# A transformer and hybrid block on one core: POOL's second feed-forward block waits for DVE's last low row, and the last stage's rows and second weight block are moved

## The chip, the cores and the metric

One core of a Trainium2 chip. The metric is the device time of one execution in microseconds; three executions of the kernel before took 4351.44, 4353.88 and 4355.54 us (median 4353.88). Engines: PE (TensorE, matmul), PEld (its weight load), DVE (VectorE), ACT (ScalarE), POOL (GpSimd) and SP (SyncE, here a queue of loads only).

## The reference

Input x has 512 tokens of 1024 channels, fp32. Four layers come first, each a mixer (hyena, window attention, pool, hyena) and a feed-forward:

```python
x = x + y
x = x + swiglu(rmsnorm(x, norm_ffn[i]), ff_w_gate[i], ff_w_up[i], ff_w_down[i])
# swiglu: (silu(xn @ wg) * (xn @ wu)) @ wd, hidden width 2816
```

Then one block with gated delta rule heads and latent attention, merged, and at its end a modulated squared-relu MLP:

```python
x = x + mod_x[5] * _sq_relu_mlp(_modulate(_rms(x, norm_mlp[l]), mod_x[3], mod_x[4]), w_mlp_in[l], w_mlp_out[l])
# _modulate(xn, shift, scale) = xn * (1.0 + scale) + shift;  _sq_relu_mlp: square(relu(h @ w1)) @ w2
```

## The kernel before, in words

x lies in SBUF with channels on the partitions: DT = 8 rows of [128, 512]. All stages follow one list (hyena, feed-forward and so on); each engine has its own program over that list, in which every instruction is issued in order and waits on semaphores. The order is written out by hand.

**Split products.** The large layers are computed with two rounded parts of each operand. A value v has a high part (v rounded to fp32r) and a low part (v less the high part), and PE adds three matmuls per tile pair (`split_product`, L954 to L956; `split_pair` L965 to L967 for a stage's first block): high weights times high rows, high weights times low rows, low weights times high rows. Weights come in blocks of [128, 2048] (output blocks are narrower) through a ring of four slots, loaded by SP (L597) as slots come free. For each block ACT copies the ring slot into `w_hi` (`split`, L1891), then POOL subtracts into `w_lo` (L808), both with two buffers, chosen by j % 2; PE waits for `wlo_set` before it uses the block. SP's load for a slot waits for the `wlo_set` of the block that was in it.

**A feed-forward's start.** The mixer's last layer writes eight output tiles. For each, DVE adds the tile to x (`residual`: L2565, L2567 or L2569), ACT makes the high row `x_hi` with the norm's gain (L1911, Identity with a per-partition scale) and the square for the norm (L1907), DVE the low row `x_lo` (`scaled_low`, L2502, a scalar_tensor_tensor, signals `xn_set`) and the running sum of the squares (`fold`, L2534). Behind its squares 4 and 5 ACT issues the split of the stage's weight blocks 0 and 1 (L1926, L1928). POOL splits block 0 as soon as its high part is there. Block 1 (j == 1) also waits until PE has finished the mixer's last tile (`acc_full`). DVE's last instructions are: the last tile into x, low row 6, low row 7, the fold of square 6.

PE goes through the first block row by row, two tiles side by side, six matmuls a row, and waits for `xn_set` at each row. Behind row 2 it issues the column sums of the squares (L927 on the folded tile, which waits for the last fold, and L931), behind row 5 the spread of the norm's factor over the tokens (L938).

**The last stage** (`modulate(1)`, then `mlp`). The output layer of the merge runs 16 matmuls a tile (L918), `gated_residual` (L3293) adds each tile to x, ACT takes the squares, with the split of block 0 behind square 4. There is no fold of the gain here: the factor must be known before the rows. So the column sums, the root and the spread come first; then DVE makes for each row k the product with gain and factor (L2880, scalar_tensor_tensor), adds the shift in place (L2881, tensor_scalar), ACT copies the high row (L1898, signals `xhi_set`), and DVE subtracts for the low row of k - 1 (`low`, L2497). ACT's program issues the split of block 1 only at the start of `mlp` (L2428), behind its eight high rows:

```python
for f in range(DT):
    if f % 2 == 0:
        ends.append(acc.n + 2)
        j += 1
        split("mlp", 0, j)
    t = full(acc, acc_full)
```

From then on each input block lasts 48 matmuls on PE, each output block 24, and ACT and POOL prepare the next one meanwhile.

Of the kernel before, what the change touches and what calls it, by code (L numbers as in the profile page):

```python
# [18 lines left out]
DT = D // P  # L19
# [270 lines left out]
def build_program(nc, stream, vecs, tabs, tabs2, x_in, ctx_in, first_mods, scratch, x_keep, diag, solved_t, solved_n, out, schedule):  # L290
# [4 lines left out]
    with ExitStack() as stack:  # L295
# [450 lines left out]
        def _(pool):  # L746
# [50 lines left out]
            def split(stage, blocks_):  # L797

                def run_(arg):
                    first = starts[(stage, arg)]  # L800
                    for j in range(blocks_):
                        k = first + j
                        cols = blocks[k][2]
                        n["split"] += 1
                        pool.wait_ge(whi_set, n["split"])
                        if stage == "ffn" and j == 1:
                            pool.wait_ge(acc_full, n["acc"])
                        nc.gpsimd.tensor_tensor(w_lo[:, j % 2, 0:cols], ring[:, k % RING, 0:cols], w_hi[:, j % 2, 0:cols],  # L808
                                                ALU.subtract).then_inc(wlo_set, 1)
                    if stage == "ffn":  # L810
                        n["aux"] += 2
                        n["acc"] += 2 * (FT + DT)
                return run_
# [1039 lines left out]
        def _(act):  # L1853
# [59 lines left out]
            def norm(gain, then=None):  # L1913

                first = acc.n - DT
                if gain is not None and gain[0] == "norm_ffn":
                    then = ("ffn", gain[1] // DT)
                ffn_next = gain is not None and gain[0] == "norm_ffn"
                for k in range(n["squared"], DT):
                    if ffn_next:  # L1920
                        scaled(k, first + k, gain)
                    if first >= 0:
                        square(k, first + k)
                    else:
                        signal(go(xn[:, k, :], x[:, k, :], ACT.Square), squares_set)
                    if then and k == 4:  # L1926
                        split(*then, 0)
                    if k == 5 and ffn_next:  # L1928
                        split(*then, 1)
                    if k == DT - 2 and first >= 0 and split_target(gain) == "hyena":  # L1930
                        high_weights(starts[("hyena", gain[1] // DT // 3)], in_hi[0])
                    if k == DT - 2 and split_target(gain) == "attention":
                        high_weights(starts[("attention", 0)], at_whi[:, 0, :])
                n["squared"] = 0
                step(go(small_t[:, 26:27], one_col, ACT.Sqrt))
                t = aux.take()
                aux.take()
                act.wait_ge(aux_drained[aux.place(t)], aux.turn(t) + 1)
                signal(go(rstd_col, rstd_col, ACT.Sqrt, bias=eps_col, scale=1.0 / D), root_set)
                if split_target(gain) == "hyena":  # L1940
                    if first < 0:
                        high_weights(starts[("hyena", gain[1] // DT // 3)], in_hi[0])
                    split_x(x_hi_h)
                if split_target(gain) == "attention":
                    split_x(x_hi_a)
                if then and not ffn_next:
                    split_x(x_hi)

            def ffn(layer):
                n["xn"] += DT  # L1950
# [469 lines left out]
            def mlp(_):  # L2420
                ends.clear()
                j = 0
                for part in range(4):
                    for f in range(DT):
                        if f % 2 == 0:
                            ends.append(acc.n + 2)
                            j += 1
                            split("mlp", 0, j)  # L2428
                        t = full(acc, acc_full)
                        if f >= 2:  # L2430
                            act.wait_ge(hidden_set, DEPTH * FT + DT * part + f - 1)
                        drain(go(h_tmp[:, f % 2, :], bank(t)[:], ACT.Relu), t)
                    for m in range(DT):
                        acc.n += 1
                        ends.append(acc.n)
                        j += 1
                        if j < 6 * DT:
                            split("mlp", 0, j)
# [25 lines left out]
        def _(dve):  # L2464
# [34 lines left out]
            def scaled_low(k, gain):  # L2499
                n["xhi"] += 1  # L2500
                dve.wait_ge(xhi_set, n["xhi"])
                signal(stt(x_lo[:, k, :], x[:, k, :], V(gain[0], gain[1] + k), x_hi[:, k, :], ALU.mult, ALU.subtract), xn_set)  # L2502

            def split_hidden(f):

# [365 lines left out]
            def modulate(which):  # L2871
# [5 lines left out]
                    step(tt_(gm[:, c, :], gm[:, c, :], gain, ALU.mult))  # L2877
                t, rows = rstd_rows()
                for k in range(DT):
                    step(stt(xn[:, k, :], x[:, k, :], gm[:, 0, k:k + 1], rows, ALU.mult, ALU.mult))  # L2880
                    signal(ts_(xn[:, k, :], xn[:, k, :], modv[:, shift + k, 0:1], None, ALU.add), plain_set if which else xn_set)  # L2881
                    if which and k:
                        low(k - 1)
                rows_read(t)
                if which:
                    low(DT - 1)
                n["xn"] += DT
                if which == 0:
                    n["sq"] += DT
# [661 lines left out]
```

## Time and profile before

| what | value |
| --- | --- |
| median of three executions | 4353.88 us |
| the profiled execution | 4356.94 us |
| its span in the profile | 4355.1 us |
| mean granted clock of PE | 0.953 of full speed |
| PE busy | 4128.2 us (95%) |
| DVE busy | 2225.0 us (51%) |
| POOL busy | 1495.2 us (34%) |
| ACT busy | 1270.7 us (29%) |

Busy times are sums over the whole span. PE's matmuls overlap, so its busy time is not work at its peak, and stretches in which its granted clock is low count as busy as well. The feed-forwards start near 448, 1073, 1492 and 2285 us, the last stage's block 0 at 3984 us.

### The profile page before, as it was taken

The numbers are of one execution on the slowest core, as the hardware profiler recorded it, in microseconds if no ns is written. First come the engines' busy times: TensorE is split into PE (matmuls) and PEld (weight loads), VectorE is DVE, ScalarE is ACT, GpSimd is POOL, SyncE is SP. The second block draws the span as 40 slices with busy tenths as digits, with TensorE's granted clock in tenths as the row PEclk, the third lists the DMA queues.
The fourth block names the chain that finished last, engine by engine and source line by source line (L and its number), as shares of the span: only waits on it lengthen the run. The fifth ranks groups of instructions, "written<-read, shape, count | busy, mean of one in ns | idle before, by whom it ended". The sixth has DMA issues, their size and how long they took to land.

```text
span 4355.1 us, 48965 instructions
## 1 busy us (share of the span) xinstructions
PE 4128.2 (95%) x19446; PEld 3130.2 (72%) x19446; DVE 2225.0 (51%) x3169; ACT 1270.7 (29%) x1756; POOL 1495.2 (34%) x845
## 2 busy tenths in 40 slices
PE   7998999999999999999989999899999999998999
PEld 6655888777888888876568886566666665775887
DVE  6588435476514441575875244556663356404322
ACT  3332222355222322233322222323221234412222
POOL 3311344321444244433124441466663000331343
PEclk9998999999999899999989998989998889999999
DMA  6201332311232223222013321111111111221222
GB/s 184 98 29 39 110 108 82 111 46 55 95 118 83 85 79 120 92 71 94 29 49 124 116 80 66 43 41 54 39 36 54 70 72 65 78 93 62 92 103 76
DMA packets 101075, 341.94 MB, mean 79 GB/s; under 512 B 44400, under 2 KB 47600, under 8 KB 72176
## 3 DMA queue, kind: packets, MB, share of 16 engines
q1 hardware_dynamic: 87968, 311.60, 20.5%
q10 hardware_dynamic: 12880, 27.20, 2.2%
q8 instruction: 155, 2.54, 0.2%
q14 instruction: 72, 0.59, 0.0%
HBM read 321.48 MB, written 17.30 MB: 78 GB/s over the span
## 4 chain that ended last, share of the span: by engine, by line
PE 83%; DVE 11%; ACT 2%; POOL 2%; issue 1%; DMA 0%; SPq 0%; DVEq 0%; ACTq 0%; POOLq 0%
PE bank L954 17%; PE bank L955 17%; PE bank L956 17%; PE bank L1454 5%; PE bank L1166 2%; PE bank L1078 1%; PE bank L1434 1%; PE bank L1156 1%; PE bank L1074 1%; PE bank L918 1%; PE bank L1755 1%; PE bank L1754 1%; PE bank L1776 1%; PE bank L1686 1%; PE bank L1715 1%
## 5 line engine op out<-in xcount | busy, mean ns | idle before, releaser
L808 POOL TENSOR_TENSOR w_lo<-ring,w_hi 128x2048 fp32r<-128x2048 f32 (+2 forms) x200 | 776.2, 3881 | 1214.6 <-ACT w_hi L1891 1193.9
L954 PE MATMUL bank<-x_hi,w_hi 128*128 128x512 f32 x1584 | 617.7, 390 | 7.5 <-POOL w_lo L808 7.5
L956 PE MATMUL bank<-x_hi,w_lo 128*128 128x512 f32 x1584 | 616.6, 389 | 0.0
L955 PE MATMUL bank<-x_lo,w_hi 128*128 128x512 f32 x1584 | 616.4, 389 | 0.0
L1891 ACT ACTIVATE w_hi<-ring 128x2048 fp32r<-128x2048 f32 (+2 forms) x200 | 322.0, 1610 | 712.9 <-PE bank L956 712.0
L954 PE MATMUL bank<-h_hi,w_hi 128*128 128x512 f32 x960 | 374.0, 390 | 0.4
L955 PE MATMUL bank<-h_lo,w_hi 128*128 128x512 f32 x960 | 373.6, 389 | 0.0
L956 PE MATMUL bank<-h_hi,w_lo 128*128 128x512 f32 x960 | 373.5, 389 | 0.0
L954 PEld LDWEIGHTS bank<-x_hi,w_hi 128*128 128x128 f32 x1584 | 297.4, 188 | 70.2 <-POOL w_lo L808 9.2
L956 PEld LDWEIGHTS bank<-x_hi,w_lo 128*128 128x128 f32 x1584 | 297.4, 188 | 61.9
L955 PEld LDWEIGHTS bank<-x_lo,w_hi 128*128 128x128 f32 x1584 | 297.4, 188 | 61.6
L821 POOL TENSOR_TENSOR ring_r<-ring,merge_hi 128x2048 fp32r<-128x2048 f32 x16 | 73.3, 4584 | 497.4 <-ACT merge_hi L2403 497.4
L1454 PE MATMUL bank<-xn,ring 128*128 128x512 f32 x496 | 238.9, 620 | 1.4 <-DVE work L2924 1.4
L2569 DVE TENSOR_TENSOR x<-bank,x 128x512 f32<-128x512 f32 x72 | 49.8, 692 | 356.8 <-PE bank L956 345.3
L954 PEld LDWEIGHTS bank<-h_hi,w_hi 128*128 128x128 f32 x960 | 180.2, 188 | 39.3 <-DVE h_lo L2508 2.1
L956 PEld LDWEIGHTS bank<-h_hi,w_lo 128*128 128x128 f32 x960 | 180.3, 188 | 37.5
L955 PEld LDWEIGHTS bank<-h_lo,w_hi 128*128 128x128 f32 x960 | 180.2, 188 | 37.1
L1966 ACT ACTIVATE xn<-xn 128x512 f32<-128x512 f32 x88 | 55.7, 633 | 455.9 <-DVE xn L2582 455.8
L793 POOL TENSOR_TENSOR tab<-tab 56x31 f32<-56x31 f32 (+15 forms) x248 | 155.1, 626 | 19.4
L2582 DVE TENSOR_TENSOR xn<-bank,rstd_t 128x512 f32<-128x512 f32 x88 | 60.8, 691 | 194.0 <-PE bank L956 187.3
L1454 PEld LDWEIGHTS bank<-xn,ring 128*128 128x128 f32 x496 | 92.6, 200 | 89.9 <-issue 88.7
L845 POOL TENSOR_TENSOR work<-work,ring 128x1024 f32<-128x1024 f32 x32 | 76.8, 2432 | 228.4 <-DVE x L2635 171.6
(527 smaller groups left out, 7934.0 us busy)
## 6 DMA issues: line engine op xcount, KB each, us to landing
ring<-stream SPq DMA_DIRECT2D x211, 1024.0 KB, 4.8
ring<-stream SPq DMA_DIRECT2D x64, 704.0 KB, 4.0
ring<-stream SPq DMA_DIRECT2D x36, 512.0 KB, 3.4
xn<-first_mods SPq DMA_DIRECT2D x8, 1024.0 KB, 6.9
x<-x_keep ACTq DMA_DIRECT2D x3, 2048.0 KB, 8.8
ring<-stream SPq DMA_DIRECT2D x4, 1088.0 KB, 4.9
bias_rows<-work ACTq DMA_DIRECT2D x1, 4096.0 KB, 46.5
x_keep<-x ACTq DMA_DIRECT2D x2, 2048.0 KB, 10.8
```

Of the source, the lines that this page charges most:

```text
L793: solve(tt(W[:, 0:i, i:SUB], W[:, 0:i, i:SUB], part, ALU.subtract))
L808: nc.gpsimd.tensor_tensor(w_lo[:, j % 2, 0:cols], ring[:, k % RING, 0:cols], w_hi[:, j % 2, 0:cols], ALU.subtract).then_inc(wlo_set, 1)
L821: nc.gpsimd.tensor_tensor(ring_r[:, w, 0:2 * DT * P], ring[:, w, 0:2 * DT * P], merge_whi[j % 2][:], ALU.subtract).then_inc(wlo_set, 1)
L845: nc.gpsimd.tensor_tensor(pair, pair, factor[:, r:r + 1, :].broadcast_to([P, 2, 512]), ALU.mult).then_inc(filt_set, 1)
L954: mm(b[:], hi[:, at + k, :], rhs_hi, start=(k == 0), stop=False)
L955: mm(b[:], hi[:, at + k, :], rhs_lo[:, k, :], start=False, stop=False)
L956: ins = mm(b[:], lo[:, at + k, :], rhs_hi, start=False, stop=(k == kt - 1))
L1166: ins = mm(b[:], fwd[term], filt[:, kind, term[1], :], start=(j == 0), stop=(j == 1))
L1454: ins = mm(b[:, 0:TC] if ctx else b[:], w[:, at + k, :], src[:, k, :], start=(k == 0), stop=(k == DT - 1))
L1891: signal(go(w_hi[:, j % 2, 0:cols], ring[:, k % RING, 0:cols], ACT.Copy), whi_set)
L1966: signal(go(gate_tmp[:, f % 2, :], gate_tmp[:, f % 2, :], ACT.Silu), silu_set)
L2582: drain(tt_(gate, bank(t)[:], rstd, ALU.mult), t)
```

## The change

Four edits. POOL's split of block 1 of each feed-forward waits in addition for all low rows of that layer (`xn_set` at 8 * (2 * layer + 2)). In the last stage ACT's split of block 1 is issued behind square 5 of the residual, as in the feed-forwards, and no longer at the start of `mlp`. DVE no longer adds the shift: ACT's high row is an Identity activation with the shift as its bias, rounded to fp32r, and DVE's low row is a scalar_tensor_tensor (row plus shift, less the high row). `modulate(0)` keeps its two instructions a row.

```diff
--- before.py
+++ after.py
@@ -805,6 +805,7 @@
                         pool.wait_ge(whi_set, n["split"])
                         if stage == "ffn" and j == 1:
                             pool.wait_ge(acc_full, n["acc"])
+                            pool.wait_ge(xn_set, DT * (2 * arg + 2))
                         nc.gpsimd.tensor_tensor(w_lo[:, j % 2, 0:cols], ring[:, k % RING, 0:cols], w_hi[:, j % 2, 0:cols],
                                                 ALU.subtract).then_inc(wlo_set, 1)
                     if stage == "ffn":
@@ -1925,7 +1926,7 @@
                         signal(go(xn[:, k, :], x[:, k, :], ACT.Square), squares_set)
                     if then and k == 4:
                         split(*then, 0)
-                    if k == 5 and ffn_next:
+                    if k == 5 and then:
                         split(*then, 1)
                     if k == DT - 2 and first >= 0 and split_target(gain) == "hyena":
                         high_weights(starts[("hyena", gain[1] // DT // 3)], in_hi[0])
@@ -1944,7 +1945,10 @@
                 if split_target(gain) == "attention":
                     split_x(x_hi_a)
                 if then and not ffn_next:
-                    split_x(x_hi)
+                    for k in range(DT):
+                        n["plain"] += 1
+                        act.wait_ge(plain_set, n["plain"])
+                        signal(go(x_hi[:, k, :], xn[:, k, :], ACT.Identity, bias=modv[:, 3 * DT + k, 0:1]), xhi_set)
 
             def ffn(layer):
                 n["xn"] += DT
@@ -2425,7 +2429,8 @@
                         if f % 2 == 0:
                             ends.append(acc.n + 2)
                             j += 1
-                            split("mlp", 0, j)
+                            if j > 1:
+                                split("mlp", 0, j)
                         t = full(acc, acc_full)
                         if f >= 2:
                             act.wait_ge(hidden_set, DEPTH * FT + DT * part + f - 1)
@@ -2500,6 +2505,11 @@
                 n["xhi"] += 1
                 dve.wait_ge(xhi_set, n["xhi"])
                 signal(stt(x_lo[:, k, :], x[:, k, :], V(gain[0], gain[1] + k), x_hi[:, k, :], ALU.mult, ALU.subtract), xn_set)
+
+            def shifted_low(k, shift):
+                n["xhi"] += 1
+                dve.wait_ge(xhi_set, n["xhi"])
+                signal(stt(x_lo[:, k, :], xn[:, k, :], modv[:, shift + k, 0:1], x_hi[:, k, :], ALU.add, ALU.subtract), xn_set)
 
             def split_hidden(f):
 
@@ -2877,13 +2887,17 @@
                     step(tt_(gm[:, c, :], gm[:, c, :], gain, ALU.mult))
                 t, rows = rstd_rows()
                 for k in range(DT):
-                    step(stt(xn[:, k, :], x[:, k, :], gm[:, 0, k:k + 1], rows, ALU.mult, ALU.mult))
-                    signal(ts_(xn[:, k, :], xn[:, k, :], modv[:, shift + k, 0:1], None, ALU.add), plain_set if which else xn_set)
-                    if which and k:
-                        low(k - 1)
+                    ins = stt(xn[:, k, :], x[:, k, :], gm[:, 0, k:k + 1], rows, ALU.mult, ALU.mult)
+                    if which:
+                        signal(ins, plain_set)
+                        if k:
+                            shifted_low(k - 1, shift)
+                    else:
+                        step(ins)
+                        signal(ts_(xn[:, k, :], xn[:, k, :], modv[:, shift + k, 0:1], None, ALU.add), xn_set)
                 rows_read(t)
                 if which:
-                    low(DT - 1)
+                    shifted_low(DT - 1, shift)
                 n["xn"] += DT
                 if which == 0:
                     n["sq"] += DT
```

## Rows read from the trace of the kernel before

**Rows 1.** Page, part 4: the chain that ended last, shares of the span by engine.
```profile
PE 83%; DVE 11%; ACT 2%; POOL 2%; issue 1%; DMA 0%; SPq 0%; DVEq 0%; ACTq 0%; POOLq 0%
```
**Rows 2.** What PE waited for: us in total, times, longest us.
```profile
PE bank L927 <- DVE xn L2534: 34.5, 10, 15.9
...
PE bank L954 <- POOL w_lo L808: 7.5, 4, 3.5
```
**Rows 3.** Timeline of PE at three feed-forward starts: start us, us, instruction [idle before].
```profile
452.11 0.39 PE L967 MATMUL bank<-x_hi,w_lo 128*128 128x512 f32 x1
455.69 1.02 PE L927 MATMUL bank<-ones,xn 128*128 128x1 f32 x8 [3.19 <-DVE xn L2534]
...
1499.58 1.02 PE L927 MATMUL bank<-ones,xn 128*128 128x1 f32 x8 [1.35 <-DVE xn L2534]
...
2291.80 1.02 PE L927 MATMUL bank<-ones,xn 128*128 128x1 f32 x8 [2.87 <-DVE xn L2534]
```
**Rows 4.** Stretches: length, busy us per engine, granted clock, DMA share, GB/s.
```profile
457.50:461.20 3.70, 3.70 (x11) 2.89 (x12) 0.50 (x3) 0.30 (x1) 0.00 (x0) 0.54 0.34 102
...
2653.00:3731.00 1078.00, 992.55 (x5784) 689.28 (x5783) 601.99 (x1326) 325.23 (x621) 377.83 (x549) 0.90 0.17 53
...
3952.00:3958.50 6.50, 6.50 (x16) 2.85 (x15) 1.44 (x2) 2.54 (x2) 2.09 (x1) 1.00 0.00 0
...
4002.60:4021.00 18.40, 18.39 (x81) 15.21 (x82) 12.29 (x13) 3.72 (x4) 9.43 (x2) 1.00 0.17 58
```
**Rows 5.** Timeline of DVE at the first feed-forward start.
```profile
443.71 0.75 DVE L2502 SCALAR_TENSOR_TENSOR x_lo<-x,vec,x_hi 128x512 fp32r<-128x512 f32 x1
...
449.29 5.52 DVE L2502 SCALAR_TENSOR_TENSOR x_lo<-x,vec,x_hi 128x512 fp32r<-128x512 f32 x2
454.85 0.69 DVE L2534 TENSOR_TENSOR xn<-xn 128x512 f32<-128x512 f32 x1
```
**Rows 6.** Timeline of POOL at the first feed-forward start.
```profile
448.89 4.59 POOL L808 TENSOR_TENSOR w_lo<-ring,w_hi 128x2048 fp32r<-128x2048 f32 x1 [7.62 <-PE bank L956]
```
**Rows 7.** Chain in order of time, last stage's start: start us, us, what.
```profile
3980.50 0.76 DVE xn L2880
...
3983.84 0.76 DVE xn L2880
3984.62 0.50 DVE xn L2881
3985.14 0.70 DVE x_lo L2497
...
3996.03 1.93 ACT w_hi L1891
3998.03 4.54 POOL w_lo L808
```
**Rows 8.** Timeline of PE at the last stage's start.
```profile
3983.95 0.77 PE L965 MATMUL bank<-x_hi,w_hi 128*128 128x512 f32 x1 [3.55 <-DVE x_lo L2497]
...
4002.61 0.50 PE L954 MATMUL bank<-x_hi,w_hi 128*128 128x512 f32 x1 [3.53 <-POOL w_lo L808]
```
**Rows 9.** ACT's groups by shape: busy us, mean ns.
```profile
L1911 ACT ACTIVATE x_hi<-x,vec 128x512 fp32r<-128x512 f32 x32 | 23.2, 724 | 46.1 <-DVE x L2567 26.3 <-DVE x L2565 12.1 <-DVE x L2569 7.4
```
**Rows 10.** Timeline of DVE, a feed-forward start and a head's stage.
```profile
1095.79 0.69 DVE L2508 TENSOR_TENSOR h_lo<-xn,h_hi 128x512 fp32r<-128x512 f32 x1
...
2905.05 0.74 DVE L2997 SCALAR_TENSOR_TENSOR work<-bank,work 128x128 f32<-128x128 f32 x2
2905.82 0.62 DVE L2965 TENSOR_SCALAR work<-work,vec 128x772 f32<-128x772 f32 x1
```
**Rows 11.** Timeline of POOL at the same two places.
```profile
1095.81 5.16 POOL L808 TENSOR_TENSOR w_lo<-ring,w_hi 128x2048 fp32r<-128x2048 f32 x1 [17.74 <-ACT w_hi L1891]
...
2905.94 1.64 POOL L783 TENSOR_TENSOR x<-x,tab 128x512 f32<-128x512 f32 x1 [14.60 <-DVE work L2997]
```
**Rows 12.** Timeline of ACT ahead of the last stage.
```profile
3967.49 0.63 ACT L1907 ACTIVATE xn<-x 128x512 f32<-128x512 f32 x1 [6.24 <-DVE x L3293]
```

## The prediction

> **What bounds the kernel now.** The page comes first. The chain that ended last is 83% PE and 11% DVE [rows 1], so a microsecond is worth something only where PE has nothing to issue or runs at half clock. The list of PE's waits names the two places that the change touches [rows 2]: L927, the first matmul of the column sums, has waited 34.5 us for DVE's fold (L2534) in ten places, and L954, the product on a low weight block, 7.5 us for POOL in four.
>
> The timeline of PE splits the first sum [rows 3]. The ten include the four feed-forward starts, each after 18 matmuls of the first block: 3.19, 2.84, 1.35 and 2.87 us, together 10.25. Behind each wait PE falls to half clock: at the first start the granted clock is 0.54 from 457.5 to 461.2 us, which is almost all 1.2 instead of 2.4 GHz [rows 4].
>
> DVE's timeline says why the fold is late [rows 5]. A low row (L2502) takes 0.75 us undisturbed (443.71), but the pair at 449.29 takes 5.52, and the fold only starts at 454.85. POOL's timeline gives the holder: its split of block 1 (L808) starts at 448.89 and takes 4.59, to 453.48 [rows 6]; the two operations with both inputs in SBUF don't run together. The same pattern stands at the other three starts.
>
> In the last stage the chain shows DVE at three instructions a row and then, in series, ACT's high part of block 1 (3996.03), POOL's low part (3998.03, 4.54) and PE's L954 at 4002.61, which has waited 3.53 us [rows 7, 8].
>
> **Feed-forward starts, four times: the added wait.** It keeps POOL off until low row 7 is written. Worked out at the first start: low row 6 runs 449.29 to 450.04. ACT's high row 7 cannot start before x is written at 449.26; with 0.72 us for an L1911 [rows 9] and about 0.06 for each hand-over it ends near 450.07, low row 7 runs 450.13 to 450.88, the fold 450.92 to 451.61. PE issues its 18th matmul at 452.11 and is free at about 452.35 [rows 3], 0.7 us after the fold. So all of the wait goes; the third start, with the shortest wait, has over 2 us of room by the same working. Gain: 10.25.
>
> What queues behind the new wait: on POOL only the splits of blocks 2 and later, whose high parts come 18 us later. Block 1 would be done at about 451 + 5.2 = 456.2. PE needs it after 30 more matmuls, the column sums and the spread: before at 466.9, now near 462 (an estimate, 466.9 less the gain below). SP's fifth load waits for that split too, but PE uses that block some 40 us on (each block lasts 48 times 0.23, 11 us). The cover is 5 us; without it each microsecond of lateness would cost one.
>
> **Who takes the port.** The new risk is the moment itself: low row 7 releases POOL's 4.6 us split and DVE's own fold together. Nearest rows [rows 10, 11]: L2997 ended at 2905.79, DVE's next instruction started at 2905.82 and the one of POOL that waited for L2997 at 2905.94, so DVE was first by 0.12. Six hand-overs in this trace are of this kind and all leave DVE ahead by 0.1; in nine others POOL starts 0.06 to 0.09 after the end of DVE's instruction, and DVE's own next, where nothing else holds it, comes after 0.04. With a lead of only 0.02 (1095.79 against 1095.81) DVE kept its 0.69 us and POOL took 5.16 instead of 4.6. I take: the fold first, POOL 0.6 longer, at no cost; both ends stay (rival B).
>
> **The clock behind the waits.** Eight or nine matmuls step 0.43 instead of 0.23 us after each of the four column sums; at the first start 457.5 to 461.2 holds 3.7 us of half clock [rows 4], in which half the time is lost: about 1.7; the others measure 1.55, 1.5 and 1.57 by the same count. Sum 6.3. Will it go? The column sums themselves (1.8 us of one-column matmuls) remain, the idle time before them does not. Below: nothing is regained, 0. Above: 6.3. For the upper end speaks that PE stood still for 3.53 us at 3999 and still had a granted clock of 1.00 afterwards [rows 4, 8]; against it, that at the third start 1.35 us of waiting plus the sums was enough. What stood before each of the four falls was the wait and the sums; with the wait gone only the sums are left. I take 6.3, the value of the rows on which PE keeps working.
>
> **Last stage, the rows.** Now: L2880 0.75, L2881 0.49, L2497 0.69 and gaps, 1.93 in work and 2.03 us a row with three gaps [rows 7]. After: L2880 0.75 and a scalar_tensor_tensor with two SBUF inputs for the low row; the nearest row is L2502 at 0.75 [rows 5]. With two gaps of 0.04 that is 1.57 a row. ACT's copy becomes an Identity with a per-partition operand, 0.72 as L1911 [rows 9]: it fits into 1.57. The profile's table loads stand at six lines, and none is an Identity's, so none is added. Start: L2880 of row 0 ends at 3981.25, ACT 3981.34 to 3982.06, low row 0 3982.12 to 3982.87, PE from 3983.02 instead of 3983.95 [rows 8]. Low rows then end 1.57 apart, row 7 near 3993.3. PE, at half clock for its first seven matmuls as now (3.1 us), one step of 0.27, then 40 of 0.2275, is free at 3995.5; its row 6 would begin at 3992.8, low row 6 is ready at 3992.5. So PE, not DVE, bounds this piece by 0.3 us; before, it was free at about 3999, 4002.61 less the wait.
>
> **Last stage, block 1.** Its high part now goes into ACT's gap behind the sixth square: ACT stands idle 6.24 us before 3967.49 [rows 12], and 3961.3 + 1.9 = 3963.2. The block has landed by then: the second output block releases its slot, and no DMA moves from 3952 to 3958.5 [rows 4]; the next load is that of block 2. POOL has it at 3967.8. It may hold the fold that starts at 3967.43 for 0.4 us, which the 5.4 us to the next tile hide. So PE goes from block 0 to block 1 at 3995.5 instead of 4002.61: 7.1, where 3.5 is the floor (the wait alone) and 7.5 the ceiling. Block 2 follows: ACT from about 3996.9, POOL done by 4003.5, PE needs it at 4006.4.
>
> **Sum.** 10.25 + 6.3 + 7.1 = 23.7 us off the profiled execution's 4356.94 (span 4355.1, 1.8 around it): 4333.2. That execution lies 3.06 above the median of the three shown; against 4353.88 it is 4330.2.
>
> **Rivals.**
> A, the clock stays low: only the waits go. For it speaks the third start, against it the idle 3.53 us without a fall. Gain 10.25 + 7.1 = 17.4: 4336.5. The Trainium skill, "TensorE: Matmul & The Clock Gate", Part 1, has the clock follow how busy PE has been; by that rule the sums alone might not hold the clock up, and this rival is what it would give. No row here has the sums without a wait before them.
> B, POOL gets the port before the fold. Then the fold ends 0.7 after a split that starts at 450.97 and ends at 455.57: 456.3 against 455.54 now. By the same working the four starts lose 0.75 + 1.0 + 1.05 + 1.05 = 3.9, the last stage keeps its 7.1: 4350.7. It decides if POOL is released less than 0.04 us after DVE's row; [rows 10, 11] speak against it. The Trainium skill, "SBUF — State Buffer", section "SBUF: two separate sides", has the one that starts first hold the shared port pair for its whole instruction. By that rule either order is possible here and the second pays the whole of the other's time; the trace agrees with the rule (5.52 for two rows of 0.75 behind a running split), and what decides between B and the main case is the 0.04 alone.
> C, the wait does nothing (the count is already reached at its place): only the 7.1 remains, 4346.8. The count of the rows, 16 a layer, speaks against it.
> D, slower: the half clock of the heads' stages. From 2653 to 3731 the granted clock is 0.90 [rows 4], so some 215 of 1078 us run at half clock, by bursts and waits whose place moves with everything before. To turn 23.7 of gain into a loss over 8.7, 32 us must come from there, which is 65 more us at half clock, granted clock 0.87 instead of 0.90. That point is 4363. The three times shown lie within 4.1 us, which speaks against such a swing.
>
> **How the numbers follow.** Main case 0.74, A 0.13, B 0.07, C 0.03, D 0.03. The range from 4325 (a low row a little cheaper, the runs' own scatter of 4 us) to 4342 holds the main case and A with that scatter; B, C and D are left out. A measurement can tell 0.2%, 8.7 us: the main case and A are faster, B and C the same, D slower.
>
> **What would show it.** After: at the four starts L927 has no wait for L2534, the two L2502 at the end 0.75 each, the fold 0.69 and the split behind it near 5.2; the matmuls after the column sums 0.23 apart (A: 0.43). L2880 followed by a low row every 1.57 us; the second split near 3963; L954 of block 1 without a wait for POOL. Wrong would be a fold of 4 us or more (B), a split beside the last low rows as now (C), or a longer stretch from 2653 to 3731 with a lower granted clock (D).

## The result and the profile after

The kernel takes 4323.15 us (median of three executions, 4320.36 to 4326.44) against 4353.88: a ratio of 0.9931 [0.9917, 0.9944], 30.7 us less. The forecast was 23.7 us less, 4330.2, with a range from 4325; the direction and the mechanism came out as forecast, the size did not: the time lies below the range. The profiled execution took 4323.15 us, its span is 4321.3 us, PE's mean granted clock 0.957 (before 0.953). Two executions of the experiments, 8133.07 us (the kernel before, experiment 10) and 7977.36 us (one of the eleven of experiment 6), took nearly twice as long as all the others and enter no ratio below.

The names of the lines move: L927 is now L928, L954 is L955 and L965 L966, the low row of a feed-forward L2507, the fold L2544, POOL's split L809, the last stage's product L2890 and its new low row L2512.

The chain of the page (part 4), of the changed kernel, against [rows 1]: PE has a point more of it, DVE a point less.

```profile
PE 84%; DVE 10%; ACT 2%; POOL 2%; issue 1%; DMA 0%; SPq 0%; DVEq 0%; ACTq 0%; POOLq 0%
```

PE's waits in the changed kernel (us in total, times, longest us), against [rows 2]:

```profile
PE bank L928 <- DVE xn L2544: 23.9, 6, 15.5
...
PE bank L955 <- POOL w_lo L809: 3.9, 3, 1.3
...
PE bank L966 <- DVE x_lo L2512: 2.7, 1, 2.7
```

The column sums waited 34.5 us in ten places and now 23.9 in six: the four feed-forward starts have left the list. The low weights cost 7.5 us in four places and now 3.9 in three; the longest, 3.5, is gone.

At the first start, DVE's timeline (start us, us, instruction, in brackets the idle time before it and what ended it), against [rows 5], with the second start behind it:

```profile
443.26 0.75 DVE L2577 SCALAR_TENSOR_TENSOR x<-bank,vec,x 128x512 f32<-128x512 f32 x1 [3.33 <-PE bank L957]
444.05 1.64 DVE L2507 SCALAR_TENSOR_TENSOR x_lo<-x,vec,x_hi 128x512 fp32r<-128x512 f32 x2
445.72 0.69 DVE L2544 TENSOR_TENSOR xn<-xn 128x512 f32<-128x512 f32 x1
...
1065.51 1.64 DVE L2507 SCALAR_TENSOR_TENSOR x_lo<-x,vec,x_hi 128x512 fp32r<-128x512 f32 x2
1067.18 0.69 DVE L2544 TENSOR_TENSOR xn<-xn 128x512 f32<-128x512 f32 x1
```

POOL's timeline at the same two starts, against [rows 6], and at the last stage:

```profile
446.21 4.65 POOL L809 TENSOR_TENSOR w_lo<-ring,w_hi 128x2048 fp32r<-128x2048 f32 x1 [10.20 <-DVE x_lo L2507]
...
1067.31 4.99 POOL L809 TENSOR_TENSOR w_lo<-ring,w_hi 128x2048 fp32r<-128x2048 f32 x1 [4.28 <-DVE x_lo L2507]
...
3936.35 4.52 POOL L809 TENSOR_TENSOR w_lo<-ring,w_hi 128x2048 fp32r<-128x2048 f32 x1 [2.35 <-ACT w_hi L1892]
```

The last pair of low rows takes 1.64 instead of 5.52 us and the fold follows at once. The last low row ends at 1067.15 at the second start; the fold starts 0.03 later and POOL 0.16 later, and the fold keeps its 0.69; it is POOL's split that stretches (4.99 against 4.59). At the first start POOL comes about 0.5 behind and hardly stretches.

PE's timeline at the first start, against [rows 3]: no bracket on the column sums, which follow the 18th product directly, and steps of 0.23 us behind them.

```profile
446.85 0.39 PE L968 MATMUL bank<-x_hi,w_lo 128*128 128x512 f32 x1
447.08 0.94 PE L928 MATMUL bank<-ones,xn 128*128 128x1 f32 x8
447.89 1.03 PE L932 MATMUL bank<-ones,xn 128*128 128x1 f32 x8
448.78 0.48 PE L966 MATMUL bank<-x_hi,w_hi 128*128 128x512 f32 x1
449.10 0.39 PE L967 MATMUL bank<-x_lo,w_hi 128*128 128x512 f32 x1
...
3956.13 0.77 PE L966 MATMUL bank<-x_hi,w_hi 128*128 128x512 f32 x1 [2.67 <-DVE x_lo L2512]
...
3969.04 0.39 PE L955 MATMUL bank<-x_hi,w_hi 128*128 128x512 f32 x1
```

The last two of these rows are the last stage: the start waits 2.67 us instead of 3.55, and block 1 follows block 0 without the 3.53 us of [rows 8]. Stretches of the changed kernel (length, busy us of PE, PEld, DVE, ACT and POOL, granted clock, DMA share, GB/s): the column sums and what follows at the first start, then block 0 of the last stage in two parts.

```profile
447.00:449.00 2.00, 2.00 (x19) 1.96 (x18) 0.00 (x0) 0.01 (x1) 2.00 (x1) 1.00 0.19 78
449.00:452.60 3.60, 3.60 (x17) 2.93 (x17) 0.50 (x3) 0.30 (x1) 1.86 (x1) 1.00 0.43 109
3956.10:3960.10 4.00, 3.97 (x9) 3.15 (x10) 3.82 (x6) 1.54 (x3) 0.00 (x0) 0.50 0.00 0
3960.10:3969.00 8.90, 8.90 (x40) 7.39 (x39) 5.91 (x9) 3.18 (x5) 0.00 (x0) 0.99 0.00 0
```

At the first start the clock stays at 1.00 (2.4 GHz), where it was 0.54 before [rows 4]. Block 0 of the last stage still has its cold beginning, 4.0 us at 1.2 GHz.

DVE's rows in the last stage, changed kernel, against [rows 7]: product and low row, one pair every 1.57 us.

```profile
3955.24 0.75 DVE L2512 SCALAR_TENSOR_TENSOR x_lo<-xn,modv,x_hi 128x512 fp32r<-128x512 f32 x1
3956.02 0.75 DVE L2890 SCALAR_TENSOR_TENSOR xn<-x,gm,bank 128x512 f32<-128x512 f32 x1
3956.81 0.75 DVE L2512 SCALAR_TENSOR_TENSOR x_lo<-xn,modv,x_hi 128x512 fp32r<-128x512 f32 x1
```

**Where the time went.** PE issues the same 19,446 matmuls in every trace here (a kernel with spare matmuls has these more), so two traces can be laid side by side by the number of the matmul. A start is the stretch from the first matmul of a feed-forward's block 0 to the matmul 114 later. Worked out from the records of the two traces, in us:

| stretch | before | after |
| --- | --- | --- |
| up to start 1 | 432.35 | 427.47 |
| start 1 | 28.19 | 23.16 |
| start 2 | 27.86 | 23.16 |
| start 3 | 27.86 | 24.75 |
| start 4 | 27.89 | 23.20 |
| the rest of each of the four feed-forwards | 342.37 | 342.37 |
| norm and attention mixer | 254.36 | 255.99 |
| norm and pool mixer | 49.11 | 49.01 |
| norm and second hyena | 421.97 | 421.89 |
| norm ahead of the heads | 5.75 | 5.04 |
| heads' stage | 591.16 | 586.26 |
| merge's output layer and norm | 65.75 | 64.85 |
| last stage, block 0 until block 1 | 18.66 | 12.91 |
| the rest of the last stage | 343.64 | 343.41 |

The four starts lose 17.5 us and the last stage 6.9 (0.90, 5.75 and 0.23), 24.4 in all, near the forecast 23.7. But these two executions lie 33.8 us apart, and the medians 30.7. The other 9.4 come mostly from two stretches in which the change does nothing, 4.9 each: the way to the first start and the heads' stage. (The stretch left out of the table, between the heads and the merge's output layer, agrees within 0.01, and the wait ahead of the first matmul differs by 0.36.) So either the change acts there in some hidden way, or a single trace isn't a fair sample. That is what the experiments had to settle.

### The profile page after: what moved, and what is told of

Read it like the earlier page. It is cut to its first block, busy times and chain, and to the rows that moved or that the text cites. A ratio compares the mean times of both kernels' runs of the same rounds, so it can differ in the third digit from the quotient of the medians.

```text
span 4321.3 us, 48957 instructions
## 1 busy us (share of the span) xinstructions
PE 4112.0 (95%) x19446; PEld 3121.2 (72%) x19446; DVE 2201.9 (51%) x3161; ACT 1271.4 (29%) x1756; POOL 1495.7 (35%) x845
## 3 DMA queue, kind: packets, MB, share of 16 engines
q8 instruction: 155, 2.54, 0.2%
## 4 chain that ended last, share of the span: by engine, by line
PE 84%; DVE 10%; ACT 2%; POOL 2%; issue 1%; DMA 0%; SPq 0%; DVEq 0%; ACTq 0%; POOLq 0%
PE bank L955 17%; PE bank L956 17%; PE bank L957 17%; PE bank L1455 5%; PE bank L1167 2%; PE bank L1079 1%; PE bank L1435 1%; PE bank L1157 1%; PE bank L1075 1%; PE bank L919 1%; PE bank L1756 1%; PE bank L1755 1%; PE bank L1777 1%; PE bank L1687 1%; PE bank L1716 1%
## 5 line engine op out<-in xcount | busy, mean ns | idle before, releaser
L809 POOL TENSOR_TENSOR w_lo<-ring,w_hi 128x2048 fp32r<-128x2048 f32 (+2 forms) x200 | 776.9, 3885 | 1189.4 <-ACT w_hi L1892 1158.5
L955 PE MATMUL bank<-x_hi,w_hi 128*128 128x512 f32 x1584 | 617.4, 390 | 3.9 <-POOL w_lo L809 3.9
L955 PE MATMUL bank<-h_hi,w_hi 128*128 128x512 f32 x960 | 373.9, 389 | 0.4
L955 PEld LDWEIGHTS bank<-x_hi,w_hi 128*128 128x128 f32 x1584 | 297.4, 188 | 66.2 <-POOL w_lo L809 5.2
L955 PEld LDWEIGHTS bank<-h_hi,w_hi 128*128 128x128 f32 x960 | 180.2, 188 | 39.3 <-DVE h_lo L2518 2.0
L2866 DVE SCALAR_TENSOR_TENSOR kbuf<-xn,vec,kbuf 128x256 f32<-128x256 f32 x112 | 154.0, 1416 | 2.0
```

The lines of the kernel that those rows point to most:

```text
L955: mm(b[:], hi[:, at + k, :], rhs_hi, start=(k == 0), stop=False)
L2866: ins = stt(part, w[:, :, j, :], V("cond", 2 * j + c), part, ALU.mult, ALU.add)
```

## Experiments

Ratios are against the kernel before, measured beside them on the same chip, with a 95% interval in brackets; a number in brackets behind a time is the number of executions; "starts" is the sum of the four stretches of the table.

**1. The changed kernel again.** No edit.

> The changed kernel, a second time, unchanged. Theory 1 (the 7 us beyond the forecast 23.7 are the runs' own scatter in stages that the change does not touch, where PE falls to half clock at other places from one execution to the next): the ratio over five rounds comes to between 0.9935 and 0.9950 (22 to 28 us), and in the trace the 448 us ahead of the first feed-forward, where no instruction is changed, take anything between 443 and 449 us. Theory 2 (the surplus belongs to the change): the ratio stays near 0.993 (30 us) and the stages between the feed-forward starts are again shorter than in the trace before by the same amounts.

Measured: 4321.46 us (5 executions), the kernel before 4352.49 (21): 0.9927 [0.9915, 0.9940], 31.0 us less. Starts 95.1. But up to the first start its trace takes 432.43 us, as much as the first trace of before, and norm and pool mixer 42.20 instead of 49.01. The 4.9 us up to the first start are therefore scatter, and a single stretch of one execution can be off by 5 to 7 us for the same code. The ratio is below what theory 1 gives (0.9935 to 0.9950), and its interval leaves out the forecast's 0.9946: the surplus over the forecast is real, and only its place in the first two traces misled. In the pool mixer the rows show what differs, PE's clock. 12 us near the mixer's end in the first trace of the changed kernel, then the like in this one (columns as above), and what PE does behind them here:

```profile
1466.00:1478.00 12.00, 12.00 (x59) 12.00 (x58) 9.29 (x8) 7.08 (x7) 4.54 (x1) 0.50 0.01 1
...
1460.00:1472.00 12.00, 12.00 (x109) 12.00 (x110) 10.02 (x14) 8.27 (x12) 0.05 (x1) 1.00 0.05 20
...
1476.71 0.80 PE L966 MATMUL bank<-x_hi,w_hi 128*128 128x512 f32 x1 [2.54 <-POOL w_lo L809]
```

At full clock PE is through the mixer earlier and then waits 2.54 us for POOL's low part of block 0; at half clock it is later and waits for nothing.

**2. POOL's wait alone**, on the kernel before:

```diff
+                            pool.wait_ge(xn_set, DT * (2 * arg + 2))
```

> The kernel before with POOL's added wait alone. By the forecast's terms: 10.25 us of waiting and 6.3 us of half clock at the four feed-forward starts, 16.5 us, ratio 0.9962. If the clock term is worth nothing: 10.3 us, 0.9976. If the surplus of 7 us belongs to the feed-forwards: 23 us, 0.9947. In the trace the four starts have no wait of the column sums for the fold and no 0.43 us steps behind them.

Measured: 4325.61 us (5), 0.994 [0.9926, 0.9953], 26.9 us less [20.5 to 32.2]. Starts 95.5, all four without a wait for the fold. The forecast for this part was 16.5, outside the interval. The wait is the part that gives more than forecast; the 23 us that were named for a surplus in the feed-forwards fit (the starts of experiments 3, 4 and 10 sum to 118.3, which is 22.8 more than 95.5).

**3. Block 1's split moved alone:**

```diff
-                    if k == 5 and ffn_next:
+                    if k == 5 and then:
...
-                            split("mlp", 0, j)
+                            if j > 1:
+                                split("mlp", 0, j)
```

> The kernel before with only the last stage's second weight split behind the residual's sixth square. Its 3.53 us wait for POOL goes, DVE's pace stays 2.03 us a row: 3.6 us, ratio 0.9992, not told apart from no change by the time; in the trace PE goes from block 0 to block 1 without a wait. If the two edits of the last stage need each other, nothing is gained.

Measured: 4348.68 us (11), 0.9994 [0.9985, 1.0003], 3.8 us less, which the time alone doesn't tell from no change. In the trace block 0 takes 14.96 instead of 18.66, which is 3.7, the 3.53 of the wait and little more, as the floor of the forecast said. Its trace holds the surprise: the starts, whose code is that of before, sum to 118.4 us instead of 111.8. Its stretches around the second start (columns as above): PE stands still, then the column sums, then products, then the clock is back.

```profile
1074.00:1076.90 2.90, 0.06 (x2) 0.07 (x1) 2.65 (x3) 0.00 (x0) 0.66 (x1) 1.00 0.01 3
1076.90:1079.20 2.30, 2.30 (x16) 2.30 (x17) 0.00 (x0) 0.00 (x0) 0.00 (x0) 0.74 0.00 0
1079.20:1084.90 5.70, 5.70 (x15) 4.50 (x16) 0.50 (x3) 0.30 (x1) 0.00 (x0) 0.51 0.55 213
1084.90:1090.00 5.10, 5.10 (x28) 4.32 (x27) 1.38 (x2) 0.00 (x0) 0.00 (x0) 1.00 0.90 376
```

The clock falls during the column sums already (0.74) and stays near 1.2 GHz for 5.7 us more: 12 steps of 0.43 us, where the first trace had 7 at this start. PE's timeline of the same place shows the sums themselves slowed: the second eight of them, 1.03 us in the first trace of after, take 1.64 here.

```profile
1076.86 1.02 PE L927 MATMUL bank<-ones,xn 128*128 128x1 f32 x8 [2.85 <-DVE xn L2535]
1077.75 1.64 PE L931 MATMUL bank<-ones,xn 128*128 128x1 f32 x8
```

**4. The shift alone:** ACT's high row with its bias and `shifted_low`, both as in the change, and neither the wait nor the moved split.

```diff
-                    split_x(x_hi)
+                    for k in range(DT):
...
+                        signal(go(x_hi[:, k, :], xn[:, k, :], ACT.Identity, bias=modv[:, 3 * DT + k, 0:1]), xhi_set)
```

> The kernel before with only the shift moved into ACT's rounding. Low rows every 1.57 us instead of 2.03; the last high row is done some 3.5 us earlier and ACT's and POOL's split of block 1 behind it as well, so PE starts block 1 3.6 us earlier, with the wait for POOL still about 3.5 us: 3.6 us, ratio 0.9992. If the chain through POOL hid all of it, 0.

Measured: 4347.75 us (11), 0.9990 [0.9981, 0.9998], 4.7 us less; in the trace 0.90 ahead of block 0 and 2.73 in it, 3.6. Its PE timeline in the last stage shows why no more: block 1 still waits for POOL.

```profile
3977.55 0.77 PE L965 MATMUL bank<-x_hi,w_hi 128*128 128x512 f32 x1 [2.67 <-DVE x_lo L2510]
...
3993.48 0.50 PE L954 MATMUL bank<-x_hi,w_hi 128*128 128x512 f32 x1 [2.85 <-POOL w_lo L808]
```

The two edits of the last stage remove different time (3.7 and 3.6; together 6.9), so neither stands in for the other. The starts here: 118.3. By their medians the three parts give 26.9 + 3.8 + 4.7 = 35.4 us, the whole 31.0; each of them is uncertain by some 4 to 6 us, so no interplay can be read from that.

**5. The clock without the wait's removal.** The kernel before, with 12 spare matmuls on tiles that are there already, issued ahead of the column sums, so that PE works while it waits. The fold is as late as before.

```diff
-            def column_sums():
+            def column_sums(fill=0):
...
+                for _ in range(fill):
+                    mm(b[:], w_hi[:, 0, 0:P], x_hi[:, 0, :], start=True, stop=True)
...
-                split_layers(2, FT // 2, FT // 2, True, {2: column_sums, 5: rstd_spread})
+                split_layers(2, FT // 2, FT // 2, True, {2: lambda: column_sums(12), 5: rstd_spread})
```

> The kernel before, POOL's split where it was, but PE issues 12 spare matmuls (2.7 us) into the column sums' bank while it waits for the fold at each of the four feed-forward starts. The wait's length stays, only PE's idle time is taken out of it, so the difference to the kernel before is the price of the clock alone (less 1.4 us at the third start, where the fill is longer than the wait). The forecast's clock term, 6.3 us in all: 5 us faster, ratio 0.9989. The rival that the first four single runs suggest (two traces without the wait added have 29.5, 31.2 and 29.5 us at starts 2 to 4 where the first trace has 27.9, half clock lasting 13 matmuls and not 8): 12 to 14 us faster, 0.997. If the column sums alone bring the clock down: no difference.

Measured: 4345.67 us (11), 0.9981 [0.9972, 0.9990], 8.5 us less [4.4 to 12.2], although the fold comes as late as before and no column sum starts more than 0.1 us earlier in its block. Starts 109.3 against 118.3. PE's timeline at the second start: the spare matmuls cover the wait, and the sums are not slowed.

```profile
1074.02 2.88 PE L925 MATMUL bank<-x_hi,w_hi 128*128 128x512 f32 x12
1076.98 1.05 PE L929 MATMUL bank<-ones,xn 128*128 128x1 f32 x8
1077.89 1.03 PE L933 MATMUL bank<-ones,xn 128*128 128x1 f32 x8
```

This is the clock's price by itself, and not all of it: at the first start 0.41 us of waiting is left and 7 slow steps follow, and at the third the spare matmuls last longer than the 1.35 to 1.68 us that they cover. By the time alone the 6.3 of the forecast is not excluded; the stretches are clearer. Starts 2 and 4, where the waits are covered, take 26.20 and 26.19 instead of 29.50 and 29.44: 3.3 us of clock each, where the forecast had 1.6.

**6. Rival B provoked.** The changed kernel, POOL released by low row 6 instead of 7:

```diff
-                            pool.wait_ge(xn_set, DT * (2 * arg + 2))
+                            pool.wait_ge(xn_set, DT * (2 * arg + 2) - 1)
```

> The changed kernel with POOL released by low row 6 instead of low row 7, so that its split is issued while row 7 runs and the fold comes behind it. If who is first at the port decides (rival B's mechanism), the fold takes 4.5 us or more at all four starts, the column sums wait again, and the time goes back by 20 us or more, to 4341 or above. If DVE's queued instruction keeps the port against POOL, the time stays at that of the changed kernel.

Measured: 4354.19 us (11; 4353.84 without the long one), 0.9997 [0.9987, 1.0006]: the starts' gain is gone. DVE's and POOL's timelines at the first start:

```profile
444.76 1.64 DVE L2507 SCALAR_TENSOR_TENSOR x_lo<-x,vec,x_hi 128x512 fp32r<-128x512 f32 x2
446.44 4.91 DVE L2544 TENSOR_TENSOR xn<-xn 128x512 f32<-128x512 f32 x1
```
```profile
446.04 4.76 POOL L809 TENSOR_TENSOR w_lo<-ring,w_hi 128x2048 fp32r<-128x2048 f32 x1 [9.30 <-DVE x_lo L2507]
```

Here the split began 0.40 us ahead of the fold, and the fold took 4.91 instead of 0.69: that is rival B. It is so at this start only. At the other three the split comes behind low row 6 and catches low row 7, and the fold behind it takes its 0.69. DVE's and POOL's timelines at the second start:

```profile
1070.94 5.13 DVE L2507 SCALAR_TENSOR_TENSOR x_lo<-x,vec,x_hi 128x512 fp32r<-128x512 f32 x1
1076.11 0.69 DVE L2544 TENSOR_TENSOR xn<-xn 128x512 f32<-128x512 f32 x1
```
```profile
1070.97 4.56 POOL L809 TENSOR_TENSOR w_lo<-ring,w_hi 128x2048 fp32r<-128x2048 f32 x1 [3.40 <-DVE x_lo L2507]
```

By the records row 7 began 0.03 us before the split, and yet it is the row that was held (5.13 instead of 0.75) while the split took its usual time; starts 3 and 4 are alike. So a recorded lead of 0.03 us doesn't say who gets the port, though one of 0.02 went to DVE in [rows 10, 11].

PE waited 3.51, 3.65, 2.15 and 3.66 us for the fold: starts 120.2, 1.9 above the usual ones of before (below), while block 0 of the last stage keeps its 12.87. By these two the kernel should still be 5 us faster than before; the interval, 5.7 faster to 2.6 slower, holds that and the forecast of rival B (4350.7). The second hyena layer takes 427.94 in this trace, where the others have 421.9 to 425.0, and that was not followed up. The Trainium skill, "SBUF — State Buffer", section "SBUF: two separate sides", lets the engine that starts first hold the shared ports for its whole instruction; the rows of the first start agree, and so do the undisturbed fold and the stretched split of the changed kernel. At the other three starts one instruction waited for the whole of the other too, but the recorded starts have the order the other way round by 0.03 us.

**7. A small wait given back.** The changed kernel, with four spare copies on DVE before the last low row, which makes the fold 1.8 us later:

```diff
+                    for _ in range(4):
+                        step(nc.vector.tensor_copy(rstd, x[:, 0, :]))
```

> The changed kernel with four spare copies of 128x512 (0.43 us each) on DVE ahead of low row 7 at each feed-forward start, so that the fold comes about 1.9 us later and PE waits about 1.2 us at starts 1, 2 and 4 and not at 3. If a short wait is charged at its own length: 3.7 us slower than the changed kernel. If it brings the clock down too, as 1.35 us of waiting did at the third start before: 1.6 to 3.3 us more at each of three starts, 9 to 14 us slower, and 0.43 us steps behind the column sums in the trace.

Measured: 4326.66 us (5), 0.9942 [0.9930, 0.9955], 5.2 above the changed kernel's 4321.46 (3.5 where each is set against the kernel before of its own call), with starts at 101.9 instead of 95.1. That is between the two forecasts, 3.7 for the waits alone and 9 to 14 with the clock. PE's timeline at the second start: a wait of 0.97 us, the sums, and then from 1073.67 on steps of 0.43 us (durations 0.63 instead of 0.39).

```profile
1070.41 1.02 PE L928 MATMUL bank<-ones,xn 128*128 128x1 f32 x8 [0.97 <-DVE xn L2544]
1071.30 1.03 PE L932 MATMUL bank<-ones,xn 128*128 128x1 f32 x8
...
1073.42 0.46 PE L968 MATMUL bank<-x_hi,w_lo 128*128 128x512 f32 x1
1073.67 0.63 PE L966 MATMUL bank<-x_hi,w_hi 128*128 128x512 f32 x1
```

At starts 2 and 4, waits of 0.97 and 1.07 us cost 2.9 each (seven slow steps). At the first start 1.03 us costs only 1.3 and no step is slow. The same wait has two prices.

**8. The wait in some layers only:**

```diff
+                            if arg == 3:
+                                pool.wait_ge(xn_set, DT * (2 * arg + 2))
```

for the last layer alone, and with `if arg < 3:` for the first three.

> The kernel before with POOL's added wait in the fourth feed-forward alone. Start 4 goes from 29.5 us (two traces) to 23.2: 6.3 us. Theory 3 (the heads' stage of 586.2 instead of 589 us in three traces hangs on where PE is when it comes out of the fourth start): the heads' stage takes 586.2 again, 9 us in all, ratio 0.9979. Theory 4 (its length was scatter, or hangs on all four): 589 us or more, 6.3 us in all, 0.9985.

> The kernel before with the added wait in the first three feed-forwards. Starts 1 to 3: 5.0 + 6.3 + 5.6 = 17 us by the single-edit traces, ratio 0.9961; by the forecast's clock term 12.7 us, 0.9971. Start 4 stays at 28 to 29.5 us with 0.43 us steps. By theory 3 the heads' stage stays at 589 us; by theory 4 it may be either.

Measured: the last layer alone 4348.69 us (11), 0.9988 [0.9979, 0.9997], 6.1 less; its fourth start takes 23.20, as in the changed kernel, and its heads' stage 589.30. The first three 4334.30 us (5), 0.9961 [0.9948, 0.9973], 20.5 less; their starts are 23.18, 23.20 and 25.49, the fourth stays at 29.49, and the heads' stage takes 589.25. Together 26.6, against 26.9 for all four: the starts' gains add up, as far as the intervals tell. An effect of the last start alone on the heads' stage, which follows it, was not seen: 589.30 with the wait gone, 589.30 in the kernel before (experiment 10).

**9. One wait instead of two.** The changed kernel without `acc_full` for block 1, which the new wait implies:

```diff
-                            pool.wait_ge(acc_full, n["acc"])
                             pool.wait_ge(xn_set, DT * (2 * arg + 2))
```

> The changed kernel without POOL's wait for PE's last tile, which the wait for the low rows includes; POOL then has one wait less to go through before its split. It may start up to 0.05 us closer behind low row 7. If the fold is still first (0.04 us behind row 7): the time of the changed kernel, 0.993. If POOL comes first at some starts: 8 us slower for each, with a fold of 4.5 us in the trace.

Measured: 4320.99 us (5), 0.9928 [0.9916, 0.9941], the same as the changed kernel. DVE's and POOL's timelines at the second start:

```profile
1067.60 0.69 DVE L2543 TENSOR_TENSOR xn<-xn 128x512 f32<-128x512 f32 x1
```
```profile
1067.71 5.02 POOL L808 TENSOR_TENSOR w_lo<-ring,w_hi 128x2048 fp32r<-128x2048 f32 x1 [4.25 <-DVE x_lo L2506]
```

POOL comes 0.11 us behind the fold's start instead of 0.13 to 0.14: a wait instruction less brings it nearer by hundredths, and the fold keeps its lead at all four starts. Starts 95.1. The heads' stage takes 591.72 us here, as in the first trace of before.

**10. The kernel before, again.** No edit, for its trace.

> The kernel before once more, for its trace. If the surplus belongs to the change, starts 2 to 4 take 29.5, 31.2 and 29.5 us and the stage of the heads 589 us or more, as in the two single-edit kernels of the last stage; if it was scatter, the first trace's 27.9 three times and any value of the heads' stage.

> The kernel before, another trace, since the last one fell on an execution at half clock throughout. If the first trace was a low draw of the clock's part: starts 2 to 4 near 29.5, 31.2 and 29.5 us, 12 or more steps of 0.43 us behind the column sums at starts 2 and 4, and the heads' stage 589 us or more.

The first of these two took 8133.07 us and says nothing about the starts: PE's steps are 0.45 us instead of 0.23. The second took 4352.68 us. Its PE timeline at the second start has the wait of 2.86 us, and its starts take 28.19, 29.50, 31.14 and 29.44: 118.3 us, as in experiments 3 and 4.

```profile
1077.09 1.02 PE L927 MATMUL bank<-ones,xn 128*128 128x1 f32 x8 [2.86 <-DVE xn L2534]
```

All starts that have the original wait, over the traces that hold them (us from the first matmul of block 0 to the one 114 later, in brackets PE's wait in it):

| trace | start 1 | start 2 | start 3 | start 4 |
| --- | --- | --- | --- | --- |
| the first one of before | 28.19 (3.19) | 27.86 (2.84) | 27.86 (1.35) | 27.89 (2.87) |
| before, later | 28.19 (3.19) | 29.50 (2.86) | 31.14 (1.68) | 29.44 (2.87) |
| split alone | 28.20 (3.19) | 29.50 (2.85) | 31.16 (1.65) | 29.50 (2.87) |
| shift alone | 28.18 (3.19) | 29.46 (2.84) | 31.17 (1.66) | 29.46 (2.87) |
| wait in the last layer | 29.83 (3.20) | 29.47 (2.85) | 31.15 (1.62) | (no original wait) |
| wait in the first three | (no original wait) | (no original wait) | (no original wait) | 29.49 (2.84) |
| for comparison, changed kernel, first trace | 23.16 (0) | 23.16 (0) | 24.75 (0) | 23.20 (0) |
| changed kernel, second trace | 23.20 (0) | 23.20 (0) | 25.52 (0) | 23.18 (0) |

The trace that the forecast was read from is the low one in three of its four starts. The waits agree to 0.02 us except at the third; what differs is how long the clock stays down. The Trainium skill, "TensorE: Matmul & The Clock Gate", Part 1, says of a kernel's beginning that the number of matmuls at the lower clock differs between runs of the same kernel. These traces show the same inside a kernel, with 7 or 12 slow steps at start 2 behind the same 2.84 to 2.86 us.

## Why the prediction was right, and which term was too small

**The added wait, 10.25: right.** The fold comes first, all four waits are gone, and the margin at the first start is as worked out: the fold ends at 446.41 and PE is there at 447.08, 0.67 us later (forecast 0.7). POOL comes 0.13 to 0.14 us behind the fold's start at the later starts, as in the hand-over from L2997 of [rows 10, 11], and stretches by 0.4 instead of 0.6. Block 1 is never late. Against the usual trace the waits sum to 10.6.

**The clock behind the waits, 6.3: right in kind, too small. This is the step that failed.** The forecast said that the clock would stay up with only the column sums left, and it does. It sized the loss by eight or nine slow steps per start, counted in one execution (the rows of that execution hold seven or eight). In the traces taken later 12 or 13 follow the sums at starts 2 and 4 and 9 or 10 at start 3, and the sums themselves are slowed there (2.2 to 2.9 us instead of 1.8). The usual four starts take 118.3 us and the changed ones 94.3 and 95.1 in their two traces, a gain of 23.2 to 24.0; less 10.6 of waits this leaves 12.6 to 13.4 us for the clock, about twice the term. (The difference of 0.8 is slow steps at the third start ahead of the sums, which the added wait doesn't touch.) Against the first trace the same working gives 17.5 less 10.25, 7.3 us: the count of slow steps was short by 1.0, the execution that it was applied to by the rest. Experiment 2 measured the whole part at 26.9 [20.5 to 32.2] where 16.5 was forecast, and experiment 5 shows 3.3 us of clock at each of two starts where 1.6 was forecast. Why the clock comes back after 1.8 us lost in one execution and 3.4 in another, behind waits equal to 0.02 us, isn't shown.

**The reference point.** The forecast took its durations and its total from the same execution, as it should, but that one was below the others by 6.5 us at the starts and above them by some 4 up to the first start, 5.7 in norm and pool mixer and 2 in the heads' stage. The errors cancelled in its total, so that its nearness to the median (3.06 us) hid them; the sum against it came out well (24.4 measured between the two traces, 23.7 forecast), and the step to the median did not. With 23.2 to 24.0 for the starts and 6.9 for the last stage the sum is 30.1 to 30.9, and the two measurements gave 30.7 and 31.0. So close a match is in part luck, since stages outside this sum still differ by several us from trace to trace.

**The last stage, 7.1: right, 6.9.** The rows are 1.57 us apart and the start comes 0.90 earlier (forecast 0.93). The second split starts at 3936.35, long before it is needed, and PE goes to block 1 without a wait. Block 0 takes 12.91 us where 12.48 was forecast: nine matmuls run at 1.2 GHz, 4.0 us, not seven and 3.1. Since PE bounds this piece, that is lost in full, and 0.2 comes back behind it. Why two matmuls more are slow than in the kernel before isn't shown.

**The rivals.** A (the clock stays low) fell: granted clock 1.00 behind the sums. B (POOL first) did not happen. Its mechanism is real: at the first start of experiment 6, with POOL 0.40 us ahead, the fold was held and PE waited 3.51 us instead of 3.19. But the forecast let a lead of 0.04 us decide between B and the main case, and the other three starts of experiment 6 show that a recorded lead of 0.03 can be lost; what kept B away was the 0.13 us. C fell with the four missing waits. D fell too: the heads' stage does not get longer. It takes 586.0 to 586.3 us in three of the four traces in which all four starts are without a wait, 591.72 in the fourth (experiment 9), and 588.4 to 591.2 in the others. Whether some 3 us of this are the change's isn't settled; the sum doesn't need it. The range missed because its lower end allowed for cheaper rows and the runs' scatter, not for an error in the clock term, which was the least certain of the three.

## What to carry to other kernels

Price a wait of PE by the wait and by the clock behind it, and read the second from several executions: here 2.9 us of waiting was followed by 1.8 us of lost clock in one trace and by 3.4 in the others. Where the end of one instruction of DVE lets two others start, DVE's own next one and one of POOL, and these two can't run together, measure by how much the first leads: 0.11 to 0.14 us held here at every start, 0.03 did not at three, and one count less on the semaphore put the kernel back to 4354.19. A single profiled execution may match the median in its total and still be off by several us in each stage with opposite signs, so lay two of them side by side by the number of the instruction before trusting a small term.

## What the runs showed of the hardware that was not expected

- A wait of 0.97 to 1.07 us before the 1.8 us of one-column matmuls brought seven slow steps at two starts and none at another (experiment 7), while 3.53 us without any work in the last stage left the granted clock at 1.00 [rows 4, 8]. What PE does behind the pause (one-column sums there, full products here) is the difference that the rows show; it wasn't tested by itself.
- Work without a purpose paid: 12 spare matmuls per start made the kernel 8.5 us faster [4.4 to 12.2] (experiment 5).
- The third start has 6 to 13 slow steps ahead of its column sums even where PE doesn't wait for the fold (24.75 to 26.0 us against 23.2): the change leaves 1.5 to 3 us there. PE comes to it in one of two ways, at half clock out of the pool mixer, or at full clock with a wait of 2.54 us for POOL's low part of block 0 (experiment 1).
- A record that starts 0.03 us earlier doesn't prove that its instruction had the port first (experiment 6, starts 2 to 4).
- The same stage of the same kernel scattered more than the whole: in the two traces of the changed kernel, norm and pool mixer took 49.01 and 42.20 us, and the way to the first start 427.47 and 432.43.
